# A routed-expert stage in which scatter-adds wait for those of earlier experts, and rows of x are turned and split ahead of a block's activations

## The chip, the cores and the metric

The kernel runs on one core of one Trainium2 chip. The metric is the device time of one execution in microseconds (us), lower being better. An execution is one decoder layer for 1,032 tokens, 1,024 of a new sequence and 8 single-token samples.

## The reference, cut to what matters

The layer ends with a mixture of experts: each token goes to 8 of 64 experts, and the experts' outputs are added up per token.

```python
def swiglu(x, w_gate, w_up, w_down):
    return (jax.nn.silu(x @ w_gate) * (x @ w_up)) @ w_down
...
    top_i, top_w = route(h2, p["w_router"], p["router_bias"])
    ffn = (routed_experts(h2, top_i, top_w, p["w_exp_gate"], p["w_exp_up"], p["w_exp_down"])
           + swiglu(h2, p["w_sh_gate"], p["w_sh_up"], p["w_sh_down"]))
    x = x + g2 * ffn.reshape(B, T, D)
```

D is 1024 and an expert's hidden width (FF) is 256. `routed_experts` sorts the 8,256 assignments by expert and works on blocks of 128 rows of one expert. The rows of one block, and of all blocks of one expert, are different tokens; two experts can share a token. Everything is float32. Ahead of this the layer has a conditioned norm, an input projection, two token mixers, an output projection and the routing, which the change hardly touches.

## The kernel before, in words

`routing` (to about 1055 us) finds for every expert its number of blocks. It writes `table`, which for block i holds the number of the expert (once as it is, once cut at 63), `lists`, the rows of the tokens of each block, and `xe_d`, the normed tokens with their weights in HBM. On the chip there are 92 blocks for 64 experts, so 28 blocks are not the first of their expert.

`experts` then runs all blocks in a loop that is written out by hand for each engine. The loop's code holds four blocks, and an outer loop takes eight (SPAN). Float32 products are made of three passes of rounded parts: a value is rounded to `hi`, and `lo` is what is left. So x, the gate and up weights and the first half of the down weights each need a `hi` (written by ScalarE) and a `lo` (written by VectorE). The engines work at different blocks at the same time. In the body of block i:

- GpSimd gathers the rows of block i+4 (`gather`, L2045, HBM to one of two rooms of `xg`). It then adds block i's output `ob` to `acc_d` in HBM by an indirect DMA that accumulates (L2065). Both are on GpSimd's one queue. The add waits for `ob`, for its indices `ixs`, and for the add of block i-1 to have landed (one semaphore `added`).
- TensorE transposes the hidden rows of block i (L2107, two tiles of `sg`). It transposes the x of block i+2 (`turn`, L2083, eight tiles), makes the gate and up products of block i+1 (`up`, L2092, 24 matmuls into bank 0), and then the down product of block i: six matmuls with rounded parts (L2117) and four float32 ones (L2123). The first of the six waits for `hTe_lo` and `down_lo`.
- ScalarE copies `hTe` and `hTe_hi` (L2176, L2177), writes `x_hi` of block i+2 (`take`, L2140), applies SiLU to block i+1 (`gate`, L2163), rounds the gate weights of block i+3 (L2149), the down weights of block i+1 (L2159) and the up weights of block i+3 (L2149), and writes `ob` of block i (L2185).
- VectorE writes `wexp_lo` of the up weights of block i+2 (L2207), `hTe_lo` of block i (`turned`, L2217), `x_lo` of block i+2 (`take`, L2197), and the gather's indices `ix` (L2224). It multiplies gate by up (L2221), waits for the add of block i-2 and writes `ixs` (L2227). It takes the weight column `wcol` of block i+3 from the gathered rows (L2203), and writes `wexp_lo` of the gate weights of block i+3 and `down_lo` of block i+1 (L2213).
- SyncE loads the weights of experts to come into a ring of four, 3 MB an expert.

`Final` adds the residual and norms the result once all adds have landed.

Of the kernel before, what the change touches and what calls it, by code (L numbers as in the profile page):

```python
# [25 lines left out]
D = 1024  # L26
# [14 lines left out]
E = 64  # L41
# [56 lines left out]
def layer(nc, a, o):  # L98

    with ExitStack() as top:  # L100
# [354 lines left out]
        with ExitStack() as c5:  # L455
            def far(name, shape, dt=F32):
                return sb(name, shape, dt, c5, "right")

            wdn = far("wexp_down", [P, RING, FF // P, D])
            wexp = far("wexp", [P, RING, 2, KD * FF])  # L460
            table = far("table", [1, ITEMS + AHEAD, 2], I32)
            starts = far("starts", [1, E], I32)
            total = far("total", [1, 1], I32)
            lists = far("lists", [P, ITEMS + AHEAD], U32)
            ix = [far(f"ix{b}", [P, 1], U32) for b in range(RING)]

            xg = nc.alloc_sbuf_tensor_at("xg", [P, ROOMS, XW], F32, offset=at)
            next_stage()
            up_in = [top.enter_context(nc.semaphore(f"up_in{i}")) for i in range(RING)]
            down_in = top.enter_context(nc.semaphore("down_in"))  # L470
            gat = [top.enter_context(nc.semaphore(f"gat{b}")) for b in range(RING)]
            routing(nc, tidy, a, sb, sem, banks, ident, hT, xe_d, acc_d, table, starts, total, lists, ix, xg, gat, wexp, wdn,
                    up_in, down_in)
            trunk.close()
            next_stage()
            experts(nc, tidy, a, sb, sem, banks, ident, xe_d, acc_d, table, starts, total, lists, ix, xg, gat, wexp, wdn, up_in,
                    down_in, o, eps, x2_d, mod_d)
# [1020 lines left out]
def routing(nc, tidy, a, sb, sem, banks, ident, hT, xe_d, acc_d, table, starts, total, lists, ix, xg, gat, wexp, wdn, up_in,  # L1498
# [3 lines left out]
    with ExitStack() as ctx:  # L1502
# [57 lines left out]
        with nc.Block() as block:  # L1560
# [70 lines left out]
            def _(pe):  # L1631
# [45 lines left out]
                pe.wait_ge(past_ok, 1)  # L1677
                n = ITEMS + AHEAD
                pe.matmul(banks[7][0:1, 0:n], onesb[0:E, 0:1], past[:], start=True, stop=True)
                pe.matmul(banks[7][0:1, 500:501], nbw[:, 0:1], onesb[0:E, 0:1], start=True, stop=True).then_inc(tab_ps, 1)  # L1680

                def tokens_to_places(t):
# [69 lines left out]
            def _(dve):  # L1752
# [103 lines left out]
                n = ITEMS + AHEAD  # L1856
                s.run(dve.tensor_copy(table[:, :, 0], banks[7][0:1, 0:n]))
                s.run(dve.tensor_scalar(table[:, :, 1], banks[7][0:1, 0:n], float(E - 1), None, ALU.min))
                s.run(dve.tensor_copy(total[:], banks[7][0:1, 500:501]))
                s.run(dve.tensor_copy(lists[:, ITEMS:], idle[:].to_broadcast([P, AHEAD])))  # L1860
                for t in range(2, TILES):
# [35 lines left out]
def experts(nc, tidy, a, sb, sem, banks, ident, xe_d, acc_d, table, starts, total, lists, ix, xg, gat, wexp, wdn, up_in, down_in,  # L1897
# [3 lines left out]
    with ExitStack() as ctx:  # L1901
        def tile(name, shape, dt=F32):
# [17 lines left out]
        wcol = tile("wcol", [P, RING])  # L1920
        none = tile("none", [ROW0, D // 4])
        ixs = [tile(f"ixs{b}", [P, 1], U32) for b in range(2)]
        names = "ix ixs tp xhi xlo wc whi wlo gu sg h hp h0hi h0lo h1 dhi dlo d0 dn ob scat wu pad".split()
        (ix_ok, ixs_ok, x_tp, xhi_ok, xlo_ok, wc_ok, whi_ok, wlo_ok, gu_ps, sg_ok, h_ok, h_tp, h0hi_ok, h0lo_ok, h1_ok, dhi_ok,
         dlo_ok, d0_ps, dn_ps, ob_ok, added, up_ok, pad_ok) = (sem("s6" + n) for n in names)
        passed = sem("s6passed")
        kept_in, ended = sem("s6kept"), sem("s6ended")

        def entry(eng, i, field, top):

            return eng.value_load(table[0:1, bass.ds(i, 1), field:field + 1].rearrange("a b c -> a (b c)"),  # L1931
                                  min_val=0, max_val=top)
# [28 lines left out]
        with nc.Block() as block:  # L1961
            @block.sync
            def _(sp):
# [63 lines left out]
                sp.sem_inc(ended, 1)  # L2027
                sp.wait_ge(dn_ps, n)
                sp.sem_inc(ended, 1)
                sp.wait_ge(added, 16 * n + 32)  # L2030
                sp.sem_inc(ended, 1)
                last.sync(sp)

            @block.gpsimd
            def _(pool):
                pool.memset(none[:], 0.0).then_inc(pad_ok, 1)
                pool.wait_ge(pad_ok, 1)
                for c in range(2):
                    pool.dma_start(acc_d[0:ROW0, c * (D // 2):(c + 1) * (D // 2)].rearrange("t (j n) -> t j n", j=2),
                                   none[:].unsqueeze(1).to_broadcast([ROW0, 2, D // 4])).then_inc(added, 16)  # L2040

                tidy(pool)

                def gather(j, q):
                    pool.indirect_dma_start(out=xg[:, q % ROOMS, 0:XW], out_offset=None, in_=xe_d,  # L2045
                                            in_offset=bass.IndirectOffsetOnAxis(ap=ix[q][:, 0:1], axis=0),
                                            bounds_check=LAST_ROW, oob_is_err=False).then_inc(gat[q], 16)

                for j in range(ROOMS, AHEAD):
                    pool.wait_ge(x_tp, j - 1)  # L2050
                    pool.wait_ge(wc_ok, j - 1)
                    gather(j, j)

                def block_of(i, q):
                    b = q % 2
                    pool.wait_ge(x_tp, i + 3)
                    pool.wait_ge(wc_ok, i + 3)
                    pool.wait_ge(ix_ok, i + 1)
                    pool.sem_inc(passed, 1)
                    gather(i + AHEAD, (q + AHEAD) % RING)  # L2060
                    pool.wait_ge(ob_ok, 2 * i + 4)
                    pool.wait_ge(ixs_ok, i + 1)
                    pool.wait_ge(added, 16 * i + 32)
                    pool.sem_inc(passed, 1)
                    pool.indirect_dma_start(out=acc_d, out_offset=bass.IndirectOffsetOnAxis(ap=ixs[b][:, 0:1], axis=0),  # L2065
                                            in_=ob[:, b, :], in_offset=None, bounds_check=LAST_ROW, oob_is_err=False,
                                            compute_op=ALU.add).then_inc(added, 16)

                blocks(pool, block_of)
                n = blocks_done(pool)  # L2070
                pool.wait_ge(added, 16 * n + 32)

                for q in range(RING):
                    pool.wait_ge(gat[q], 16 * ((n + AHEAD + RING - 1 - q) // RING))

            @block.tensor
            def _(pe):
# [24 lines left out]
                def block_of(i, q):  # L2102
                    b = q % 2
                    e = entry(pe, i, 1, E - 1)
                    pe.wait_ge(h_ok, i + 1)
                    for f in range(FF // P):
                        last = pe.transpose(banks[3][:, f * P:(f + 1) * P], hh[:].rearrange("p (n f) -> p f n", f=FF // P)[:, f, :], ident[:])  # L2107
                    last.then_inc(h_tp, 1)
                    turn(i + 2, (q + 2) % RING, gathered(i, q, 2))
                    up(i + 1, 1 - b)  # L2110
                    slot = e & (RING - 1)
                    pe.wait_ge(ob_ok, 2 * i + 2)
# [23 lines left out]
            def _(act):  # L2136
# [29 lines left out]
                round_weights(0, 0)  # L2166
                take(1, 1)
                round_weights(1, 1)
                gate(0)
                round_weights(2, 0)  # L2170
                round_down(0)

                def block_of(i, q):
                    b = q % 2
                    act.wait_ge(h_tp, i + 1)
                    act.activation(h1[:], banks[3][:, P:FF], ACT.Copy).then_inc(h1_ok, 1)  # L2176
                    act.activation(h0_hi[:], banks[3][:, 0:P], ACT.Copy).then_inc(h0hi_ok, 1)  # L2177
                    take(i + 2, b)
                    gate(i + 1)
                    round_weights(i + 3, 1 - b, lambda: round_down(i + 1))  # L2180
                    act.wait_ge(dn_ps, i + 1)
                    act.wait_ge(wc_ok, i + 1)
                    act.wait_ge(ixs_ok, i + 1)
                    for half in range(2):
                        act.activation(ob[:, b, 512 * half:512 * half + 512], banks[4 + half][:], ACT.Copy,  # L2185
                                       scale=wcol[:, q:q + 1]).then_inc(ob_ok, 1)
# [5 lines left out]
            def _(dve):  # L2192
# [43 lines left out]
                take(1, 1)  # L2236
                for g in range(2):
                    rest_of_weights(e, 1, 1, g)
                gate(0)
                e = entry(dve, 2, 1, E - 1)  # L2240
                weight(e, 2, 16)
                rest_of_weights(e, 2, 0, 0)
                rest_of_down(entry(dve, 0, 1, E - 1), 0)

                def block_of(i, q):
                    b = q % 2
                    rest_of_weights(entry(dve, i + 2, 1, E - 1), i + 2, b, 1)
                    turned(i)
                    take(i + 2, b)
                    to_gather(i + AHEAD, (q + AHEAD) % RING)  # L2250
                    gate(i + 1)
                    dve.wait_ge(added, 16 * i + 16)
                    dve.sem_inc(passed, 1)
                    to_add(i, b)
                    e = entry(dve, i + 3, 1, E - 1)
                    weight(e, (q + 3) % RING, gathered(i, q, 3))
                    rest_of_weights(e, i + 3, 1 - b, 0)
                    rest_of_down(entry(dve, i + 1, 1, E - 1), i + 1)

                dve.wait_ge(added, 32)  # L2260
                blocks(dve, block_of)
                dve.wait_ge(kept_in, 16 * (TILES + 3))
                last.vector(dve)
# [149 lines left out]
```

## Time and profile before

| | us |
|---|---|
| three runs | 2059.60, 2062.68, 2064.72 |
| median | 2062.68 |
| profiled execution, its own time | 2062.64 |
| its span in the profile | 2061.0 |

One line of the profile stands for a group of instructions or for one of them. Its engine is PE (TensorE matmuls), PEld (TensorE weight loads), DVE (VectorE), ACT (ScalarE), POOL (GpSimd) or SPq (SyncE's queue). The name left of the arrow is written and those right of it are read. Square brackets at the end of a row tell how long the engine had been idle before it, and what released it; "issue" means nothing that the profile shows. Matmuls overlap, so a duration of 0.39 us stands beside a distance of 0.23 us from one start to the next. In this text distances are taken from starts.

### The profile page before, as it was taken

To read this page: it belongs to the slowest core of one execution; us is meant where nothing else is said; L and a number is where in the kernel's file an instruction comes from. 1 tells how busy PE (TensorE), PEld (TensorE's weight loads), DVE (VectorE), ACT (ScalarE), POOL (GpSimd) and SP (SyncE) were. 2 spreads that over 40 slices of the span, in tenths; PEclk is the share of its full clock that TensorE was granted. 3 is DMA by queue.
4 is the path that set the end of the run, shared out by engine and by line. 5 is a ranking of instruction groups with operands and counts; after the bars stand their busy time and mean duration, and the time that the engine had idled before them with its cause. 6 is when DMAs were issued, how large, how long until landed. Compare 5 with 4: busy or idle time off the path is not lost. (4 is left out here: it accounts for less than half of the span.)

```text
span 2061.0 us, 36898 instructions
## 1 busy us (share of the span) xinstructions
PE 1908.2 (93%) x10447; PEld 1529.1 (74%) x10449; DVE 1159.2 (56%) x1714; ACT 968.8 (47%) x1395; POOL 403.8 (20%) x335
## 2 busy tenths in 40 slices
PE   4999999899899999979789999999999999999995
PEld 3999999899787666755446777777677777777772
DVE  4113401166437335446337777777777777877775
ACT  5110111244113122121246777777777777777774
POOL 0100100111111000001102223322333322333230
PEclk9999999999899999989889999999999999999998
DMA  7211311111443665324069896998998889898964
GB/s 258 73 51 41 127 47 31 32 63 61 156 134 114 238 241 195 133 93 176 27 226 298 262 346 162 325 301 294 320 310 263 269 272 300 234 348 247 313 199 177
DMA packets 181813, 399.63 MB, mean 194 GB/s; under 512 B 22137, under 2 KB 86897, under 8 KB 181758
## 3 DMA queue, kind: packets, MB, share of 16 engines
q1 hardware_dynamic: 149166, 312.16, 42.5%
q0 software_dynamic: 31392, 82.49, 15.7%
q10 hardware_dynamic: 1200, 4.26, 0.6%
q8 instruction: 33, 0.54, 0.1%
q14 instruction: 22, 0.18, 0.0%
HBM read 350.16 MB, written 80.64 MB: 209 GB/s over the span
## 5 line engine op out<-in xcount | busy, mean ns | idle before, releaser
L2207 DVE TENSOR_TENSOR wexp_lo<-wexp,wexp_hi 128x2048 fp32r<-128x2048 f32 x189 | 432.7, 2290 | 81.5 <-ACT wexp_hi L2149 45.7
L2149 ACT ACTIVATE wexp_hi<-wexp 128x2048 fp32r x190 | 362.0, 1907 | 47.5 <-issue 45.7
L2092 PE MATMUL bank<-wexp_hi,x_hi 128*128 128x512 f32 x744 | 300.1, 403 | 3.8 <-DVE wexp_lo L2207 3.8
L2092 PE MATMUL bank<-wexp_hi,x_lo 128*128 128x512 f32 x744 | 292.0, 392 | 0.0
L2092 PE MATMUL bank<-wexp_lo,x_hi 128*128 128x512 f32 x744 | 290.7, 391 | 0.0
L2065 POOL DMA_INDIRECT acc_d<-ob,ixs x92 | 165.4, 1798 | 578.3 <-DMA acc_d<-ob,ixs 477.0
L548 PE MATMUL bank<-hT_hi,w_hi 128*128 128x344 f32 x576 | 187.5, 326 | 7.3 <-DVEq L660 7.3
L548 PE MATMUL bank<-hT_hi,w_lo 128*128 128x344 f32 x576 | 185.3, 322 | 0.0
L548 PE MATMUL bank<-hT_lo,w_hi 128*128 128x344 f32 x576 | 184.7, 321 | 0.0
L2123 PE MATMUL bank<-wexp_down,hTe 128*128 x368 | 173.2, 593 | 0.0
L2092 PEld LDWEIGHTS bank<-wexp_hi,x_lo 128*128 128x128 f32 x744 | 140.3, 189 | 31.0
L2092 PEld LDWEIGHTS bank<-wexp_hi,x_hi 128*128 128x128 f32 x744 | 140.5, 189 | 30.2 <-issue 4.2
L2092 PEld LDWEIGHTS bank<-wexp_lo,x_hi 128*128 128x128 f32 x744 | 140.8, 189 | 27.1
L2045 POOL DMA_INDIRECT xg<-xe_d,ix x94 | 131.1, 1395 | 83.9 <-DVE wcol L2203 46.7
L711 PE MATMUL bank<-hT_hi,wg_hi 128*128 128x344 f32 x384 | 129.6, 337 | 12.8 <-POOLq L118 6.7
L634 DVE TENSOR_TENSOR w_lo<-w_raw,w_hi 128x1024 fp32r<-128x1024 f32 x27 | 33.1, 1226 | 186.6 <-POOL w_hi L538 170.3
L711 PE MATMUL bank<-hT_lo,wg_hi 128*128 128x344 f32 x384 | 124.7, 325 | 0.0
L711 PE MATMUL bank<-hT_hi,wg_lo 128*128 128x344 f32 x384 | 124.5, 324 | 0.0
L2163 ACT ACTIVATE sg<-bank 128x256 f32<-128x256 f32 x93 | 35.8, 385 | 180.6 <-PE bank L2092 174.8
L2197 DVE TENSOR_TENSOR x_lo<-bank,x_hi 128x512 fp32r<-128x512 f32 x188 | 120.2, 681 | 0.6 <-ACT x_hi L2140 0.6
L2213 DVE TENSOR_TENSOR down_lo<-wexp_down,down_hi 128x1024 fp32r<-128x1024 f32 x93 | 113.4, 1219 | 4.8 <-ACT down_hi L2159 4.8
L2083 PE MATMUL bank<-ident,xg 128*128 128x128 f32 x752 | 99.6, 276 | 17.1 <-DMA xg<-xe_d,ix 11.4
(365 smaller groups left out, 3458.6 us busy)
## 6 DMA issues: line engine op xcount, KB each, us to landing
wexp<-in_w_exp_gate SPq DMA_DIRECT2D x128, 512.0 KB
wexp<-in_w_exp_up SPq DMA_DIRECT2D x128, 512.0 KB
wexp_down<-in_w_exp_down SPq DMA_DIRECT2D x128, 512.0 KB
wada<-in_w_ada SPq DMA_DIRECT2D x12, 2048.0 KB, 10.8
w_raw<-in_w_in SPq DMA_DIRECT2D x44, 512.0 KB, 3.9
gates_d<-gst POOLq DMA_DIRECT2D x48, 172.0 KB, 2.1
gate<-gates_d SPq DMA_DIRECT2D x16, 516.0 KB, 5.6
xn<-in_x_prompt ACTq DMA_DIRECT2D x8, 512.0 KB, 8.1
```

What stands on the lines that cost most here:

```text
L548: last = pe.matmul(bank, stat(k), mov(k), start=(k == 0 and x == 0), stop=(k == KD - 1 and x == 2))
L711: last = pe.matmul(banks[7][:, 0:PIECE], stat[j][:, k, :], mov[:, k, toks], start=(k == 0 and x == 0), stop=(k == KD - 1 and x == 2))
L2045: pool.indirect_dma_start(out=xg[:, q % ROOMS, 0:XW], out_offset=None, in_=xe_d, in_offset=bass.IndirectOffsetOnAxis(ap=ix[q][:, 0:1], axi ...
L2065: pool.indirect_dma_start(out=acc_d, out_offset=bass.IndirectOffsetOnAxis(ap=ixs[b][:, 0:1], axis=0), in_=ob[:, b, :], in_offset=None, bou ...
L2083: last = pe.transpose(banks[1 + k // 4][:, (k % 4) * P:(k % 4 + 1) * P], xg[:, q % ROOMS, k * P:(k + 1) * P], ident[:])
L2092: last = pe.matmul(banks[0][:].rearrange("p (g n) -> p g n", g=2), stat[:, b, k, :], mov[:, b, :, k * FF:(k + 1) * FF], start=(k == 0 and ...
L2123: last = pe.matmul(banks[4 + half][:], h1[:], wdn[:, bass.ds(slot, 1), 1, half * 512:half * 512 + 512].rearrange("p a n -> p (a n)"), star ...
L2149: act.activation(w_hi[:, b, g, :], wexp[:, bass.ds(e & (RING - 1), 1), g, :].rearrange("p a n -> p (a n)"), ACT.Copy).then_inc(whi_ok, 1)
L2163: act.activation(sg[:], banks[0][:, 0:FF], ACT.Silu).then_inc(sg_ok, 1)
L2197: dve.tensor_tensor(x_lo[:, b, at, :].rearrange("p k n -> p (k n)"), banks[1 + half][:], x_hi[:, b, at, :].rearrange("p k n -> p (k n)"), ...
L2207: dve.tensor_tensor(w_lo[:, b, g, :], wexp[:, bass.ds(e & (RING - 1), 1), g, :].rearrange("p a n -> p (a n)"), w_hi[:, b, g, :], ALU.subtr ...
L2213: dve.tensor_tensor(d0_lo[:], down_first(e), d0_hi[:], ALU.subtract).then_inc(dlo_ok, 1)
```

## The change

It has four parts.

1. **Adds.** `added` becomes two semaphores, one for the blocks with even numbers and one for those with odd ones. The table gets a third number for each block: how many blocks lie before the first block of its expert (one more matmul and one more copy in `routing`). GpSimd reads it from the table in each block. It lets an add wait only for the adds of the other parity that belong to earlier experts. The add of the same parity two blocks earlier is still waited for by VectorE ahead of `ixs`.
2. **First block.** The first half of the down weights of block 0 is rounded ahead of the first `gate` on ScalarE and on VectorE, where it was rounded last ahead of the loop.
3. **TensorE.** In a block, `turn` comes ahead of the transposes of the hidden rows.
4. **ScalarE and VectorE.** In a block, `take` comes ahead of `hTe` and `hTe_hi` on ScalarE, and ahead of `turned` (`hTe_lo`) on VectorE.

```diff
+                pe.matmul(banks[7][0:1, n:2 * n], nbw[:, 0:1], past[:], start=True, stop=True)
...
+                s.run(dve.tensor_copy(table[:, :, 2], banks[7][0:1, n:2 * n]))
...
+        added = [sem(f"s6scat{b}") for b in range(2)]
...
-                    pool.wait_ge(added, 16 * i + 32)
+                    pool.wait_ge(added[1 - b], ((entry(pool, i, 2, ITEMS) + b) >> 1) * 16 + 16)
...
-                                            compute_op=ALU.add).then_inc(added, 16)
+                                            compute_op=ALU.add).then_inc(added[b], 16)
...
                     e = entry(pe, i, 1, E - 1)
+                    turn(i + 2, (q + 2) % RING, gathered(i, q, 2))
                     pe.wait_ge(h_ok, i + 1)
...
                     last.then_inc(h_tp, 1)
-                    turn(i + 2, (q + 2) % RING, gathered(i, q, 2))
                     up(i + 1, 1 - b)
...
+                round_down(0)
                 gate(0)
                 round_weights(2, 0)
-                round_down(0)
 
                 def block_of(i, q):
                     b = q % 2
+                    take(i + 2, b)
                     act.wait_ge(h_tp, i + 1)
                     act.activation(h1[:], banks[3][:, P:FF], ACT.Copy).then_inc(h1_ok, 1)
                     act.activation(h0_hi[:], banks[3][:, 0:P], ACT.Copy).then_inc(h0hi_ok, 1)
-                    take(i + 2, b)
                     gate(i + 1)
...
+                rest_of_down(entry(dve, 0, 1, E - 1), 0)
                 gate(0)
...
-                rest_of_down(entry(dve, 0, 1, E - 1), 0)
...
                     rest_of_weights(entry(dve, i + 2, 1, E - 1), i + 2, b, 1)
+                    take(i + 2, b)
                     turned(i)
-                    take(i + 2, b)
                     to_gather(i + AHEAD, (q + AHEAD) % RING)
                     gate(i + 1)
-                    dve.wait_ge(added, 16 * i + 16)
+                    dve.wait_ge(added[b], (i - b) * 8 + 16)
```

VectorE, in a block of the loop, before. Names stand as in the list above; `x2` at the end of a row is a pair.

```order
L2207 TENSOR_TENSOR wexp_lo<-wexp,wexp_hi 128x2048
L2216 REGISTER_ALU
L2217 TENSOR_TENSOR hTe_lo<-bank,hTe_hi 128x128
L2197 TENSOR_TENSOR x_lo<-bank,x_hi 128x512 x2
L2224 ISA
L2224 COPY ix<-lists 128x1
L2221 TENSOR_TENSOR sg<-sg,bank 128x256
```

The same place of VectorE with the change, whose line numbers are 7 higher here:

```order
L2214 TENSOR_TENSOR wexp_lo<-wexp,wexp_hi 128x2048
L2203 REGISTER_ALU
L2204 TENSOR_TENSOR x_lo<-bank,x_hi 128x512 x2
L2223 REGISTER_ALU
L2224 TENSOR_TENSOR hTe_lo<-bank,hTe_hi 128x128
L2231 ISA
L2231 COPY ix<-lists 128x1
L2228 TENSOR_TENSOR sg<-sg,bank 128x256
```

The pair of `x_lo` has moved ahead of `hTe_lo`; nothing else in the block of VectorE has moved.

GpSimd, between the gather and the add of one block, with the change. L1934 is the read of the table's third number, L2068 the wait for the adds.

```order
L2050 DMA xg<-xe_d,ix 128x1088 [waits x_in4]
L2066 ISA
L1934 ISA [waits x_in3,w_ready]
L1934 TENSOR_LOAD table
L1934 ISA x2
L2068 ISA
L2070 DMA acc_d<-ob,ixs 1033x1024 [waits ss_ps]
```

Before, no load of the table stood between the two DMAs; gather and add keep their order.

## Rows read from the trace of the kernel before

**Rows 1.** The page: the span and the granted clock in 40 slices.

```profile
span 2061.0 us, 36898 instructions
...
PEclk9999999999899999989889999999999999999998
```

**Rows 2.** Transposes of hidden rows (L2107), two a block: count, duration, first and last start.

```profile
L2107 PE MATMUL bank<-ident,sg x184: 272/279/391, 1075.6 to 2001.6; 128*128 128x128 f32 x184
```

**Rows 3.** One block in order of time: start, duration, engine, line, tile.

```profile
1430.85 0.39 PE L2117 MATMUL bank<-down_hi,hTe_hi 128*128 128x512 f32 x1
...
1431.05 0.38 ACT L2163 ACTIVATE sg<-bank 128x256 f32<-128x256 f32 x1 [1.77 <-PE bank L2092]
...
1431.92 1.91 ACT L2149 ACTIVATE wexp_hi<-wexp 128x2048 fp32r x1 [0.49 <-issue]
...
1433.92 0.39 PE L2107 MATMUL bank<-ident,sg 128*128 128x128 f32 x2
1434.07 2.29 DVE L2207 TENSOR_TENSOR wexp_lo<-wexp,wexp_hi 128x2048 fp32r<-128x2048 f32 x1 [0.92 <-ACT wexp_hi L2149]
1434.15 1.04 PE L2083 MATMUL bank<-ident,xg 128*128 128x128 f32 x8
...
1436.28 1.22 DVE L2213 TENSOR_TENSOR down_lo<-wexp_down,down_hi 128x1024 fp32r<-128x1024 f32 x1
...
1437.41 2.29 DVE L2207 TENSOR_TENSOR wexp_lo<-wexp,wexp_hi 128x2048 fp32r<-128x2048 f32 x1
...
1437.95 1.10 ACT L2140 ACTIVATE x_hi<-bank 128x512 fp32r<-128x512 f32 x2
...
1439.61 0.28 DVE L2217 TENSOR_TENSOR hTe_lo<-bank,hTe_hi 128x128 fp32r<-128x128 f32 x1
...
1439.81 1.28 DVE L2197 TENSOR_TENSOR x_lo<-bank,x_hi 128x512 fp32r<-128x512 f32 x2
...
1440.51 0.39 PE L2117 MATMUL bank<-down_hi,hTe_hi 128*128 128x512 f32 x1
...
1441.01 0.14 DVE L2224 COPY ix<-lists 128x1 uint32 x1
```

**Rows 4.** Who waited for whom, 1066 to 2016 us: total, times, longest.

```profile
POOL acc_d L2065 <- DMA acc_d<-ob,ixs: 477.0, 73, 9.7
...
POOL acc_d L2065 <- ACT ob L2185: 74.8, 15, 6.0
...
PE bank L2083 <- DMA xg<-xe_d,ix: 11.4, 14, 1.9
```

**Rows 5.** Add, gather and what waits for it, in order of time.

```profile
1504.84 1.58 POOL L2065 DMA_INDIRECT acc_d<-ob,ixs  x1 [6.20 <-DMA acc_d<-ob,ixs]
1506.72 1.05 POOL L2045 DMA_INDIRECT xg<-xe_d,ix  x1 [0.31 <-issue]
...
1515.35 1.58 POOL L2065 DMA_INDIRECT acc_d<-ob,ixs  x1 [7.57 <-DMA acc_d<-ob,ixs]
1516.40 0.39 PE L2107 MATMUL bank<-ident,sg 128*128 128x128 f32 x2
...
1517.24 1.09 PE L2083 MATMUL bank<-ident,xg 128*128 128x128 f32 x8 [0.45 <-DMA xg<-xe_d,ix]
```

**Rows 6.** Around the first passage of the loop, in order of time.

```profile
1080.40 1.23 DVE L2213 TENSOR_TENSOR down_lo<-wexp_down,down_hi 128x1024 fp32r<-128x1024 f32 x1 [0.46 <-ACT down_hi L2159]
...
1086.48 0.77 PE L2117 MATMUL bank<-down_hi,hTe_hi 128*128 128x512 f32 x1 [3.97 <-issue]
```

**Rows 7.** Where VectorE comes from one passage of eight blocks to the next.

```profile
1249.71 0.73 PE L2117 MATMUL bank<-down_hi,hTe_hi 128*128 128x512 f32 x1 [2.26 <-issue]
1250.24 0.63 PE L2117 MATMUL bank<-down_lo,hTe_hi 128*128 128x512 f32 x1
...
1491.31 2.29 DVE L2207 TENSOR_TENSOR wexp_lo<-wexp,wexp_hi 128x2048 fp32r<-128x2048 f32 x1 [2.36 <-issue]
1493.52 0.28 DVE L2217 TENSOR_TENSOR hTe_lo<-bank,hTe_hi 128x128 fp32r<-128x128 f32 x1
...
1493.90 0.47 PE L2117 MATMUL bank<-down_hi,hTe_hi 128*128 128x512 f32 x1 [2.23 <-issue]
```

**Rows 8.** The last add, behind its `ob`.

```profile
2013.68 1.24 ACT L2185 ACTIVATE ob<-bank,wcol 128x512 f32<-128x512 f32 x2
2015.89 1.58 POOL L2065 DMA_INDIRECT acc_d<-ob,ixs  x1 [5.34 <-ACT ob L2185]
```

**Rows 9.** DMA over a fifth of the loop: PE, PEld, DVE, ACT, POOL, clock, DMA share, GB/s.

```profile
1786.00:1966.00 180.00, 174.51 (x782) 132.20 (x781) 136.82 (x176) 134.64 (x180) 58.67 (x37) 1.00 0.91 295
```

More of the change, by code:

```diff
@@ L460, in layer @@
             wexp = far("wexp", [P, RING, 2, KD * FF])
-            table = far("table", [1, ITEMS + AHEAD, 2], I32)
+            table = far("table", [1, ITEMS + AHEAD, 3], I32)
             starts = far("starts", [1, E], I32)
@@ L1922, in experts @@
         ixs = [tile(f"ixs{b}", [P, 1], U32) for b in range(2)]
-        names = "ix ixs tp xhi xlo wc whi wlo gu sg h hp h0hi h0lo h1 dhi dlo d0 dn ob scat wu pad".split()
+        names = "ix ixs tp xhi xlo wc whi wlo gu sg h hp h0hi h0lo h1 dhi dlo d0 dn ob wu pad".split()
         (ix_ok, ixs_ok, x_tp, xhi_ok, xlo_ok, wc_ok, whi_ok, wlo_ok, gu_ps, sg_ok, h_ok, h_tp, h0hi_ok, h0lo_ok, h1_ok, dhi_ok,
-         dlo_ok, d0_ps, dn_ps, ob_ok, added, up_ok, pad_ok) = (sem("s6" + n) for n in names)
+         dlo_ok, d0_ps, dn_ps, ob_ok, up_ok, pad_ok) = (sem("s6" + n) for n in names)
         passed = sem("s6passed")
+        added = [sem(f"s6scat{b}") for b in range(2)]
         kept_in, ended = sem("s6kept"), sem("s6ended")
@@ L2029, in _ @@
                 sp.sem_inc(ended, 1)
-                sp.wait_ge(added, 16 * n + 32)
+                sp.wait_ge(added[0], ((n + 1) >> 1) * 16 + 16)
+                sp.sem_inc(passed, 1)
+                sp.wait_ge(added[1], (n >> 1) * 16 + 16)
                 sp.sem_inc(ended, 1)
@@ L2039, in _ @@
                     pool.dma_start(acc_d[0:ROW0, c * (D // 2):(c + 1) * (D // 2)].rearrange("t (j n) -> t j n", j=2),
-                                   none[:].unsqueeze(1).to_broadcast([ROW0, 2, D // 4])).then_inc(added, 16)
+                                   none[:].unsqueeze(1).to_broadcast([ROW0, 2, D // 4])).then_inc(added[c], 16)
                 tidy(pool)
@@ L2066, in block_of @@
                                             in_=ob[:, b, :], in_offset=None, bounds_check=LAST_ROW, oob_is_err=False,
-                                            compute_op=ALU.add).then_inc(added, 16)
+                                            compute_op=ALU.add).then_inc(added[b], 16)
                 blocks(pool, block_of)
                 n = blocks_done(pool)
-                pool.wait_ge(added, 16 * n + 32)
+                pool.wait_ge(added[0], ((n + 1) >> 1) * 16 + 16)
+                pool.sem_inc(passed, 1)
+                pool.wait_ge(added[1], (n >> 1) * 16 + 16)
                 for q in range(RING):
@@ L2258, in block_of @@
                     rest_of_down(entry(dve, i + 1, 1, E - 1), i + 1)
-                dve.wait_ge(added, 32)
+                dve.wait_ge(added[0], 16)
+                dve.wait_ge(added[1], 16)
                 blocks(dve, block_of)
```

## The prediction

> **What bounds the kernel now.** I read the page first, for the span and the clock [rows 1]: TensorE is at its full 2.4 GHz nearly throughout. The change lives in the expert loop, so I then took the starts of the hidden rows' transposes, two a block [rows 2]. From the first to the last block they span 926.0 us, 91 distances from block to block. The shape of a block comes from the view in order of time [rows 3]. Let E be the end of the up product (which is when the down product of the block can start), and D the actual start of the down product. In [rows 3] both are 1430.85, and the next are 1440.51: 9.66 us of TensorE work without a wait. Starting points repeat at that distance in about half of the blocks. 91 x 9.66 = 879 us, so 47 us of the 926 are waits. By a list of all 92 blocks, made with the distances of [rows 3] as the norm, 5.5 lie in the first block [rows 6], some 17 at `turn`, where the gathered rows are late (14 waits with 11.4 us are named in [rows 4]; [rows 5] show one, 0.84 us from hidden transposes to `turn` where [rows 3] have 0.23), 12 ahead of the down product, 9 where one block gives way to the next, and the rest is clock and small change.
>
> Two things stand close behind TensorE. **The first** is the chain of the adds: 73 of the 92 waited for the add before them, 477 us in all [rows 4]. In [rows 5] one add follows the other after 10.51 us, and the gather stands behind the add on GpSimd's queue. So a late add makes a late gather, and that makes TensorE wait. **The second** is VectorE's way to `hTe_lo`, and on it the change acts most. In [rows 3] follow E = 1430.85: SiLU at 1431.05, rounding at 1431.92, `wexp_lo` at 1434.07, `down_lo`, the second `wexp_lo` at 1437.41, and `hTe_lo`, which ends at 1439.89. That is E + 9.04, against 9.66 for TensorE: 0.62 us to spare. The down product starts about 0.10 us after `hTe_lo` where that is what it waits for (1493.80 to 1493.90 in [rows 7]). In my list the time from the end of `hTe_lo` to the down product is 0.6 us or more in 34 blocks, 0.2 to 0.6 in 35, and 0.10 to 0.14, so that TensorE waited, in 23.
>
> **Part 4, x_lo ahead of hTe_lo.** The pair of `x_lo` takes 1.20 us of VectorE (1439.81 to the next start at 1441.01, [rows 3]), and `hTe_lo` now comes that much later. `x_hi` doesn't hold it up: with `take` first, ScalarE would have it done before the second `wexp_lo` ends at 1439.70, since today it begins at 1437.95 and takes 1.10 [rows 3]. `x_lo` itself is wanted a block later, so its being early is worth nothing. The down product can then start at E + 9.04 + 1.20 + 0.10 = E + 10.34. But not every block pays the whole 0.68 over 9.66. ScalarE's chain starts from E, not from D. If a block's down product is late by s, the next E is late by s as well, and the next down product has only 0.68 - s left to wait. Two neighbours together wait 0.68, so two blocks take 10.34 + 9.66 = 20.00 and one 10.00: **+0.34 us a block, 91 x 0.34 = +31 us.** Blocks whose `hTe_lo` is late already (23 of them) can't share: they pay 1.20 instead of the pair's 0.68, **23 x 0.52 = +12 us**. The upper bound is no sharing and no slack, 92 x 1.2 = 110; the lower is nothing if the pair found idle time of VectorE, for which [rows 3] leave no room between 1434.07 and 1441.01. ScalarE's part of the move costs nothing: `hTe_hi` ends 1.10 later, at about 1439.2, still ahead of the second `wexp_lo`'s end.
>
> **Part 3, turn first.** Same work. `turn` starts 0.23 us earlier, and so do its readers, which don't hurry. Where the gather is late, the hidden transposes used to run inside that wait and now come behind it: 14 waits x 0.23 = at most +3, and less, as gathers become less late.
>
> **Part 1, adds.** 28 of the 92 blocks are not the first of their expert, and only their adds are freed. Each lets the chain catch up by whatever it lags: singles fall behind by 10.51 - 9.66 = 0.85 a block, or 0.5 against the new pace of 10.00, and every second or third block is a free one. So I let nearly all late gathers go: **-17 us**, and with them 3 of the 12 us ahead of the down product, **-3**. What is late next is `hTe_lo`. The bounds are 0 (see the DMA rival) and -47 (all waits gone). The new read of the table costs GpSimd something between `ob` and the add. No row shows it there. The nearest is the 0.49 us idle of ScalarE before its rounding, where it loads from the table too [rows 3]; the other end is 0, since an add that waits for another has its load behind it. It counts once, at the last add, which had only its `ob` to wait for and began 0.97 us after that [rows 8]: **+0.5**. The matmul and the copy in routing are at most one transposed tile pair and one column copy, 0.39 + 0.14 [rows 3]: **+0.3**.
>
> **Part 2, first block.** `down_lo` of block 0 (1.23 us and 0.46 of waiting [rows 6]) leaves VectorE's way to the first down product, and `x_lo` (1.20) comes onto it: **-0.5**.
>
> **Clock.** At the change from one passage of eight blocks to the next, VectorE sometimes idles 2.4 us [rows 7]. After a 2.26 us gap TensorE went on at half its clock (0.43 us between down matmuls, 1250.24 on, against 0.23; 1.2 GHz instead of 2.4), after one of 2.23 it did not [rows 7]. These gaps become 1.2 longer, and each event costs 6 x 0.20 = 1.3 us: two more such events, **+2.5**, between 0 and 11 x 1.3 = 14. By the page "TensorE: Matmul & The Clock Gate" of the Trainium skill (section "HAM oscillation — how this bites in real kernels"), gaps of idleness put the engine back at the lower clock; by that rule each of the 11 would be a sure loss and this term its upper end.
>
> **Sum:** 31 + 12 + 2 - 20 + 0.5 + 0.3 - 0.5 + 2.5 = +28. The terms overlap (a block that waits for its gather is mostly one of the 23), so I take 5 off: **+23 us.** The profiled execution took 2062.64, practically the median of the runs (2062.68), so 2086.
>
> **The rivals.** *A: the adds were the true bound, and the kernel gets faster.* For it: the chain of adds covers 73 of 92 blocks [rows 4], and early gathers let VectorE start its work on time. It decides if the freed adds bring more than `x_lo` costs, which needs `hTe_lo` to end within E + 9.56 even with `x_lo` ahead. Gain 17 to 20 with nothing given back: 2062.6 - 18 = 2045. Against it: VectorE is late in [rows 3] though the gather was early enough, since ScalarE's rounding is what it waits for at 1434.07. *B: the two cancel or hide each other,* +-6, at 2062. This is also the case that the freed adds gain 20 and only the late blocks lose. *C: freeing adds gains nothing,* because the DMA engines are 0.91 busy [rows 9], and two adds in flight only take longer each. Then the 20 stay away: 2086 + 17 = 2103. The page "DMA: Bandwidth & Descriptors" of the Trainium skill (section "Issuing engines are not separate DMA queues") speaks for it: transfers, whoever starts them, run on the same 16 engines and interleave. Against it: at 10.00 us a block the gathers have more time anyway, so part of the gain comes even then.
>
> **How the numbers follow.** Forecast 0.66, A 0.12, B 0.10, C 0.12. A measurement of this kernel can tell about 0.3%, 6.2 us, from no change. Faster is A, 0.12; the same is B, 0.10; slower is the forecast and C, 0.78. For the range I leave out A and the upper end of C. The low end is the forecast with the gather gain doubled and the late blocks free, 2086 - 17 - 12 = 2057; the high end is C with a little less, 2102.
>
> **What would show it.** Right: the median distance of blocks rises from 9.66 to about 10.0, often as a short and a long one in turn. The down product (now L2124) waits in most blocks, 0.1 us behind `hTe_lo`, with 30 us or more in all. The adds' wait for adds falls well below 477 us, and `turn` hardly waits for the gather. Wrong: `hTe_lo` ends by E + 9.6 in most blocks; or distances of 9.66 prevail; or `turn` still waits as often as now.

## The result, and the profile after

| | before | changed |
|---|---|---|
| median | 2062.53 | 2085.84 |
| lowest to highest of 4 runs | 2059.60 to 2064.72 | 2084.25 to 2087.21 |
| span of the profiled execution | 2061.0 | 2083.1 |

The ratio is 1.0111 with a 95% interval of 1.0095 to 1.0127: the change makes the kernel 23.3 us slower. Medians in this text are of fast runs: one run of e6 (2790.98 us) and one of the kernel before beside e9 to e12 (3894.29 us) were in a far slower state and are left out.

The page of the changed kernel, and its chain of waits. The clock is as before ([rows 1]). The chain by lines no longer starts with the adds, which had 19% of the span before (the last row below is of the kernel before):

```profile
span 2083.1 us, 37459 instructions
...
PEclk9999999999899999989889999999999999999997
...
PE 39%; DMA 5%; issue 3%; DVE 1%; ACT 1%; ACTq 0%; SPq 0%; DVEq 0%; POOLq 0%; POOL 0%
PE bank L2099 21%; PE bank L2130 6%; PE bank L2124 6%; PE bank L2090 4%; DMA wexp_down<-in_w_exp_down 3%; DMA acc_d<-ob,ixs 1%; PE bank L2115 1%; PE bank L2324 1%; DMA xg<-xe_d,ix 1%; ACTq L1934 0%; DVE yy L2386 0%; PE bank L2329 0%; DVE wexp_lo L2214 0%; ACT ob L2192 0%; ACT wexp_hi L2156 0%
...
DMA acc_d<-ob,ixs 19%; PE bank L2092 9%; DMA xg<-xe_d,ix 4%; PE bank L2123 2%; PE bank L2117 2%; PE bank L2083 2%; DVEq L1931 1%; DVE wexp_lo L2207 1%; ACT wexp_hi L2149 1%; PE bank L2316 1%; ACTq L1931 0%; POOLq L1931 0%; DVE yy L2378 0%; ACT ob L2185 0%; PE bank L2107 0%
```

The hidden transposes, the counterpart of [rows 2] (count, duration, first and last start):

```profile
L2115 PE MATMUL bank<-ident,sg x184: 279/283/389, 1075.7 to 2021.0; 128*128 128x128 f32 x184
```

From the first to the last block it takes 945.3 us instead of 926.0. So 19.3 us arose in the loop, 0.1 ahead of its first hidden transposes, and 2.7 behind its last ones (62.1 us to the end of the span instead of 59.4). The distances from block to block changed as follows:

| | before | changed |
|---|---|---|
| median distance | 9.72 | 10.40 |
| below 9.75 us | 47 of 91 | 20 of 91 |
| above 10.3 us | 27 | 47 |
| down product starts 0.10 to 0.14 us behind `hTe_lo` | 23 of 92 | 60 of 92 |

From 1671 on, for instance, they run 9.7, 10.5, 9.7, 10.6, 9.7, 10.5: a long and a short one in turn. The list of who waited for whom, 1066 to 2040 us, against [rows 4]:

```profile
POOL acc_d L2070 <- issue: 314.3, 48, 9.7
POOL acc_d L2070 <- DMA acc_d<-ob,ixs: 301.2, 44, 9.0
...
PE bank L2124 <- issue: 30.4, 46, 3.4
...
PE bank L2090 <- issue: 12.0, 12, 1.8
```

L2124 is the down product: 30.4 us of waiting in 46 places, all put down to "issue" since the profile sees no single releaser of its three semaphores. L2090 is `turn`, whose 12 waits are at the ends of passages. Adds are named as waiting for adds in 44 blocks instead of 73. But GpSimd's idle time ahead of the adds has not fallen: 314.3 us of it in 48 blocks now have no releaser that the profile names (26 us in 4 blocks before). What most of these adds wait for can be read from their own `ob`: 64 of the 92 adds start at most 1.9 us behind its end, 1.7 to 1.8 us in nearly all of them, where before 17 did, 16 of them at 1.0 us. They wait for `ob` and then for the read of the table. One block in order of time shows the cause of the longer time, the counterpart of [rows 3]:

```profile
1635.00 0.39 PE L2124 MATMUL bank<-down_hi,hTe_hi 128*128 128x512 f32 x1
...
1635.20 0.38 ACT L2170 ACTIVATE sg<-bank 128x256 f32<-128x256 f32 x1 [3.05 <-PE bank L2099]
...
1636.31 1.91 ACT L2156 ACTIVATE wexp_hi<-wexp 128x2048 fp32r x1 [0.72 <-issue]
...
1638.45 2.29 DVE L2214 TENSOR_TENSOR wexp_lo<-wexp,wexp_hi 128x2048 fp32r<-128x2048 f32 x1 [1.28 <-ACT wexp_hi L2156]
...
1641.79 2.28 DVE L2214 TENSOR_TENSOR wexp_lo<-wexp,wexp_hi 128x2048 fp32r<-128x2048 f32 x1
...
1643.99 1.28 DVE L2204 TENSOR_TENSOR x_lo<-bank,x_hi 128x512 fp32r<-128x512 f32 x2
...
1645.19 0.28 DVE L2224 TENSOR_TENSOR hTe_lo<-bank,hTe_hi 128x128 fp32r<-128x128 f32 x1
...
1645.57 0.47 PE L2124 MATMUL bank<-down_hi,hTe_hi 128*128 128x512 f32 x1 [0.74 <-issue]
```

From E = 1635.00, `hTe_lo` ends at 1645.47, and the down product starts 0.10 us later, 10.57 us behind E. The prediction said 10.34. This block is 0.23 late of its own, by ScalarE's gap ahead of its rounding (0.72 us here, 0.49 in [rows 3] and in most blocks of both kernels). In most blocks `hTe_lo` ends at E + 10.25 and the down product starts at E + 10.35, as predicted. Two neighbours show how they share the wait:

```profile
1303.43 0.39 PE L2124 MATMUL bank<-down_hi,hTe_hi 128*128 128x512 f32 x1
...
1313.40 0.28 DVE L2224 TENSOR_TENSOR hTe_lo<-bank,hTe_hi 128x128 fp32r<-128x128 f32 x1
...
1313.78 0.47 PE L2124 MATMUL bank<-down_hi,hTe_hi 128*128 128x512 f32 x1 [0.52 <-issue]
...
1323.09 0.28 DVE L2224 TENSOR_TENSOR hTe_lo<-bank,hTe_hi 128x128 fp32r<-128x128 f32 x1
...
1323.56 0.39 PE L2124 MATMUL bank<-down_hi,hTe_hi 128*128 128x512 f32 x1
```

The first down product starts at its E, 1303.43. The second starts 10.35 us later, 0.68 us behind its own E (1313.10). The third waits for nothing: its E has moved back with the second, 9.78 us behind it, and its `hTe_lo` ended 0.19 us earlier. The two distances make 20.13 us, where the prediction had 20.00. From block to block the waits run 0.68, 0, 0.82, 0, 0.68, 0 there.

I compared where TensorE's steps stand further apart than their usual distance, summed over the loop. Ahead of the down product it is 39.1 us instead of 16.1 (+23.0). From the down product to the next block it is 18.0 instead of 9.2 (+8.8). Between hidden transposes, `turn` and `up` it is 2.4 instead of 18.5, without the start (-16.1). Within the down product it is 6.9 instead of 4.9 (+2.0). Together +17.7. The rest of the 19.3 is 0.01 to 0.02 us a block on the usual distances themselves.

### The profile page after: what moved, and what is told of

It is laid out like the page before. It is cut to its first block and busy times, and to the rows that moved or that the text cites. A ratio compares the mean times of both kernels' runs of the same rounds, so it can differ in the third digit from the quotient of the medians.

```text
span 2083.1 us, 37459 instructions
## 1 busy us (share of the span) xinstructions
PE 1918.8 (92%) x10449; PEld 1520.0 (73%) x10450; DVE 1160.8 (56%) x1715; ACT 968.9 (47%) x1395; POOL 377.4 (18%) x335
## 5 line engine op out<-in xcount | busy, mean ns | idle before, releaser
L2070 POOL DMA_INDIRECT acc_d<-ob,ixs x92 | 168.5, 1832 | 615.5 <-issue 314.3
L2090 PEld LDWEIGHTS bank<-ident,xg 128*128 128x128 f32 x752 | 86.8, 142 | 74.1 <-issue 73.6
L2050 POOL DMA_INDIRECT xg<-xe_d,ix x94 | 102.0, 1085 | 92.7 <-DVE ixs L2234 34.3
L2090 PE MATMUL bank<-ident,xg 128*128 128x128 f32 x752 | 99.5, 276 | 18.4 <-issue 12.0
```

What stands on the lines that cost most here:

```text
L2090: last = pe.transpose(banks[1 + k // 4][:, (k % 4) * P:(k % 4 + 1) * P], xg[:, q % ROOMS, k * P:(k + 1) * P], ident[:])
```

## The experiments

Three theories stood at the start. **Theory 1**: `x_lo` ahead of `hTe_lo` on VectorE costs, the freed adds gain. **Rival 2**: the new wait with its table read, or `turn` first, costs. **Rival C** of the prediction: freed adds gain nothing, because the DMA engines are full. Each comparison has runs of the kernel before on the same chip.

| run | what it is | median, us | ratio to before, 95% interval |
|---|---|---|---|
| e1 | changed, VectorE's order back | 2051.74 | 0.9958 (0.9944 to 0.9972) |
| e2 | before, VectorE's order alone | 2087.68 | 1.0130 (1.0113 to 1.0148) |
| e3 | before, adds alone | 2053.06 | 0.9960 (0.9941 to 0.9980) |
| e4 | changed, adds back | 2085.81 | 1.0118 (1.0102 to 1.0135) |
| e5 | changed, half of `x_lo` ahead | 2064.95 | 1.0011 (1.0000 to 1.0022) |
| e6 | changed, half an `x_lo` more ahead | 2113.12 | 1.0252 (1.0226 to 1.0278) |
| e7 | before, TensorE's order alone | 2064.33 | 1.0011 (0.9998 to 1.0024) |
| e8 | parts 1 and 2, `hTe_lo` first | 2055.27 | 0.9956 (0.9940 to 0.9971) |
| e9 | parts 1 and 2 | 2049.93 | 0.9930 (0.9902 to 0.9959) |
| e10 | before, `hTe_lo` first | 2062.35 | 0.9989 (0.9973 to 1.0005) |
| e11 | e9, gather ahead of the add | 2051.48 | 0.9937 (0.9912 to 0.9963) |
| e12 | e11, `hTe_lo` first | 2047.75 | 0.9922 (0.9892 to 0.9952) |

The runs of before had medians of 2061.31 (e1 to e4), 2062.12 (e5 to e8) and 2064.4 (e9 to e12).

**e1, VectorE's order back in the changed kernel.**

```diff
                     rest_of_weights(entry(dve, i + 2, 1, E - 1), i + 2, b, 1)
-                    take(i + 2, b)
                     turned(i)
+                    take(i + 2, b)
```

> The changed kernel with VectorE's order alone as before: hTe_lo ahead of x_lo. Theory 1 (x_lo ahead of hTe_lo on VectorE is what costs): the 39 us of waits ahead of the down product fall to about 12, most distances from block to block go back to 9.66 us, and the freed adds show their gain: 2040 to 2055 us. Rival 2 (the adds' new wait and table read, or turn first on TensorE, are what costs): stays within 5 us of 2086. Rival 3 (half and half): about 2070.

2051.74 us, 34 us under the changed kernel (32 by the two ratios, which have different runs of before), with the waits ahead of the down product at 13.1 us. In the profiles 29.6 us of it lie in the loop (915.7 us instead of 945.3) and 3.8 ahead of the loop, where e1 changes nothing. What the change costs lies in these two lines.

**e2, the same two lines alone, swapped in the kernel before.**

> The kernel before with VectorE's order alone changed: x_lo ahead of hTe_lo. Theory 1: +31 for the pairs and +12 for late blocks, less what late gathers lose at the slower pace (5 to 15): 2090 to 2100 us, and distances of 9.7 and 10.6 us in turn. Rival 2: no more than 5 us over 2062.

2087.68, 26 us over before, with ScalarE and TensorE in their old order: rival 2 is out. It came a little under the theory's range, and its list of waits shows one reason:

```profile
POOL acc_d L2065 <- DMA acc_d<-ob,ixs: 461.8, 67, 8.9
...
PE bank L2117 <- issue: 37.2, 49, 5.2
...
PE bank L2083 <- DMA xg<-xe_d,ix: 0.8, 2, 0.5
```

The adds still wait for each other in 67 blocks, yet `turn` waits 0.8 us for gathered rows instead of 11.4. The slower pace alone gives the gathers the time they need.

**e3, the adds alone (all of part 1 put into the kernel before).**

> The kernel before with part 1 alone (two semaphores, a table entry more, adds wait for those of earlier experts). Theory 1: 14 to 20 us faster than before, 2043 to 2049, with the waits of turn for gathered rows nearly gone. Theory that the DMA engines are the bound (C): within 4 us of before. Rival 2: slower than before by 5 or more.

2053.06, 8 us faster, half of what was expected. The waits for gathers did go (from 17.1 us, measured as distances, to 3.9). But the block-to-block step grew by 0.7 us and the wait ahead of the down product by 1.3. Some of what is won at the gather is lost at the next wait. In the profile the loop is 12.0 us shorter (914.0 instead of 926.0), but that run, at 2049.07 us, was one of the faster ones of six from 2046.66 to 2058.08.

**e4, the adds as before in the changed kernel.** The diff is part 1 taken out.

> The changed kernel with the adds as before: one semaphore, each add waits for the one before it. By the term of the prediction (20 us gained by freed adds whatever the rest does): 2103 us. If the slower pace of 10.0 us a block already gives the adds time: 2086 to 2092. Rival 2: faster than 2080.

2085.81 against 2085.84, and a ratio of 1.0118 against 1.0111, whose intervals overlap: the freed adds bring nothing here that can be told from noise, which could hide some 5 us. With the adds as before `turn` waits 0.5 us for gathered rows. The term of -17 us was right in size and had the wrong owner.

**e5 and e6, less and more ahead of `hTe_lo`.** These test the rule that two neighbours share the wait.

```diff
-                    take(i + 2, b)
+                    take(i + 2, b, (0,))
                     turned(i)
+                    take(i + 2, b, (1,))
```

In e6 half an `x_lo` is written once more ahead of the pair:

```diff
+                    dve.wait_ge(xhi_ok, 2 * (i + 2) + 1)
+                    dve.tensor_tensor(x_lo[:, b, 0:4, :].rearrange("p k n -> p (k n)"), banks[1][:],
+                                      x_hi[:, b, 0:4, :].rearrange("p k n -> p (k n)"), ALU.subtract).then_inc(extra, 1)
+                    dve.wait_ge(extra, i + 1)
                     take(i + 2, b)
                     turned(i)
```

> The changed kernel with the first half of x_lo ahead of hTe_lo and the second half behind it. If two neighbouring blocks share the wait: hTe_lo can end at E + 9.64, the pair waits 0.08 us instead of 0.68, so only blocks that are late already pay (about 20 x 0.5): 2058 to 2065 us, nearer to the 2052 of the order put back than to 2086. If every block pays in proportion to what stands ahead: halfway, 2069 or more.

> The changed kernel with one more x_lo half (written twice, with a wait between) ahead of hTe_lo, about 0.7 us more. Sharing: two blocks take 0.7 longer, 91 x 0.35 = 32, and late ones the whole: 2115 to 2125 us. No sharing: 91 x 0.7 = 64, 2145 or more. If VectorE had idle time left ahead of hTe_lo: 2086 to 2095.

Both are near what sharing says and far from its rivals: e5 at 2064.95, the upper end of its range, and e6 at 2113.12, 2 us under it. The hidden transposes of e6:

```profile
L2116 PE MATMUL bank<-ident,sg x184: 279/282/384, 1074.3 to 2050.0; 128*128 128x128 f32 x184
```

The loop takes 975.7 us instead of 945.3: 30.4 more, 0.33 us a block. In most blocks `hTe_lo` now ends at E + 10.98 instead of E + 10.25, 0.73 us later, so about half of what was put in is paid, and the waits run 1.40, 0, 1.40, 0. And e5, with half of the 1.2 us, costs 13 us over e1 (11 by the ratios), while the second half costs 21: the price rises once the slack is used up. In e5 `hTe_lo` ends at E + 9.65, and the waits run 0.08, 0.

**e7, TensorE's order alone.** The diff is part 3.

> The kernel before with turn ahead of the hidden transposes on TensorE, nothing else. The prediction's term: 0 to +3 us, 2061 to 2065. Rival, from the runs so far: where one passage of eight blocks gives way to the next, turn comes about 0.8 us later behind the down product than the hidden transposes did (11 places), so +6 to +9 us, 2067 to 2071.

2064.33, a ratio of 1.0011 with 1 inside the interval. The rival of 6 to 9 us is wrong; late gathers cost `turn` 15.0 us in this run. The row from the changed kernel that had suggested it is this one:

```profile
1244.77 1.09 PE L2090 MATMUL bank<-ident,xg 128*128 128x128 f32 x8 [1.77 <-issue]
```

Such gaps between passages of eight blocks also grew in e2 (from 9.2 to 16.7 us in all), which has the old order on TensorE. In e1, which has `turn` first and `hTe_lo` in time, `turn` waits 8.7 us at ends of passages, against 12.0 in the changed kernel. So the gaps go with a late `hTe_lo` and not with `turn`. Why is open: whether TensorE reads its instructions less far ahead of the loop's end when it is held up at the down product was not tried.

**e8 and e10, `hTe_lo` moved the other way**, with freed and with old adds.

```diff
-                    rest_of_weights(entry(dve, i + 2, 1, E - 1), i + 2, b, 1)
                     turned(i)
+                    rest_of_weights(entry(dve, i + 2, 1, E - 1), i + 2, b, 1)
                     take(i + 2, b)
```

> The kernel before with part 1 (adds) and part 2 (first block), and with VectorE's hTe_lo moved the other way: ahead of the second wexp_lo. Theory 1: the time between the end of hTe_lo and the down product grows from 0.6 to about 2 us, the 13 to 17 us of waits ahead of the down product fall to under 4: 2036 to 2044 us. Rival: x_lo, gate product and weight column come later on VectorE and something else waits: no faster than 2052.

> The kernel before, with hTe_lo ahead of the second wexp_lo on VectorE, adds as before. If the wait for hTe_lo was a limit of its own: 12 us faster, 2050. If it only hid the late gathers (as in e8, where its waits went and gathers at turn rose from 4 to 20 us): within 4 us of before, 2058 to 2066, with over 20 us of late gathers at turn.

`hTe_lo` now has 2.1 us to spare in most blocks, and the waits directly ahead of the down product fell to 2.5 us (e8) and 1.6 (e10). Neither gained: e8 is no faster than e9 below, which is the same kernel without this move, and e10 is as before. The rival expectation of e8 and the second one of e10 came true (20.4 us of late gathers at `turn` in e10). The list of waits of e8:

```profile
ACT down_hi L2166 <- DMA wexp_down<-in_w_exp_down: 28.8, 11, 4.4
PE bank L2090 <- DMA xg<-xe_d,ix: 14.7, 17, 2.5
PE bank L2114 <- DVE sg L2228: 12.2, 11, 1.3
```

The pace is not the reason that gathers are late here: e9 has the same median distance of 9.66 us and waits 2.6 us for them. The order on VectorE is. `hTe_lo` now holds up the second `wexp_lo`, and what stands behind that comes about 1.5 us later than in e9: `ix`, `ixs` and the gate product start 8.7, 9.1 and 8.7 us behind the hidden transposes (medians) instead of 7.1, 7.6 and 7.2. GpSimd then issues the gather 1.4 us later, 10.3 us instead of 11.4 ahead of its `turn`, and a gather takes 9.5 us to land. The later gate product `sg` holds up the hidden transposes. Down weights are waited for 28.8 us, against 24.5 in e9.

**e9, parts 1 and 2 alone.**

> The kernel before with parts 1 and 2 alone (adds, first block); TensorE, ScalarE and VectorE keep their order in a block. From e3 (adds alone, 8 us faster than before) and part 2's way to the first down product (down_lo 1.7 us earlier, x_lo not in its way): 8 to 11 us faster than before, 2051 to 2054. If turn first had been of use in e1: slower than e1's ratio of 0.9958.

2049.93. This is the change without what costs: 36 us under the changed kernel. Against e1 it lacks part 3 and ScalarE's half of part 4, and the two can't be told apart. Here the landing of every add can be read too: 19 of the 92 adds start before the one ahead of them has landed, where in e7 and e10, with the adds as before, none does. Against e3 it has part 2 more: the distance from the first to the second hidden transposes is 11.3 us instead of 15.8.

**e11 and e12, the gather ahead of the add on GpSimd's queue**, without and with `hTe_lo` first.

```diff
-AHEAD = 4
+AHEAD = 5
...
-                    pool.wait_ge(x_tp, i + 3)
-                    pool.wait_ge(wc_ok, i + 3)
-                    pool.wait_ge(ix_ok, i + 1)
+                    pool.wait_ge(x_tp, i + 4)
+                    pool.wait_ge(wc_ok, i + 4)
+                    pool.wait_ge(ix_ok, i + 2)
```

One more semaphore, `rooms`, lets TensorE release the gather of the last block, behind its own loop.

> As e9, and each gather stands ahead of the add on GpSimd's queue instead of behind it (it fetches block i+5 in body i, as soon as turn has freed the room). If late gathers come from standing behind the adds: waits of turn for gathers and of VectorE's wcol nearly vanish, 2040 to 2048 us. If they come from the DMA engines being full: no faster than e9.

> As e11, and hTe_lo ahead of the second wexp_lo on VectorE. If gathers are no longer late, VectorE's slack of 2 us at hTe_lo makes it the fastest: 91 x 9.66 = 879 for the blocks, some 15 us of ends of passages and late weights: 2028 to 2040 us. If the DMA engines are the bound: as e11 and e8, 2050.

Nothing on TensorE or VectorE is named as waiting for a gather any more in either, so late gathers did come from standing behind the adds. And still they take 2051.48 and 2047.75. Part of the reason lies behind the loop. These are GpSimd's last two instructions of the loop in e11:

```profile
2004.58 1.04 POOL L2051 DMA_INDIRECT xg<-xe_d,ix  x1 [13.04 <-issue]
2006.17 1.58 POOL L2074 DMA_INDIRECT acc_d<-ob,ixs  x1 [0.55 <-issue]
```

The gather of the last block fetches rows that nobody needs. It is released only when TensorE has left its loop, and the last add stands behind it on the queue: it starts 8.4 us behind the end of its `ob` in e11 and 6.6 in e12, against 1.7 in e9 and in e8, and the final stage waits for it. In e11 the loop is 4.0 us shorter than in e9 (910.9 instead of 914.9) and what follows it 6.9 us longer; in e12 the loop is 9.8 us shorter than in e8 and what follows it 3.3 us longer. Without this late add I estimate 2045 and 2043 us, from these differences of 6.7 and 4.9 us; that was not run. So e11 does not show that its gain failed for want of DMA. The rest of the reason is other waits. The list of e12:

```profile
POOL acc_d L2074 <- DMA acc_d<-ob,ixs: 206.8, 54, 6.3
...
ACT down_hi L2173 <- DMA wexp_down<-in_w_exp_down: 46.4, 17, 4.8
...
PE bank L2119 <- DVE sg L2235: 20.3, 20, 1.3
```

ScalarE waits 46.4 us for down weights, against 28.8 in e8 and 14.9 in the kernel before. In e11 it waits 26.6, hardly more than in e9 (24.5). A window of 900 us of e11, columns as in [rows 9]:

```profile
1066.00:1966.00 900.00, 879.69 (x3947) 673.48 (x3946) 691.87 (x896) 670.76 (x892) 267.34 (x177) 0.99 0.90 292
```

The DMA engines are 0.90 busy at 292 GB/s; in the kernel before they are 0.88 busy at 287 in the same window. Whether the weights come later in e12 because the gathers do, or are only wanted sooner at its faster pace, was not tried. By its median e12 is the fastest of all, but its interval overlaps with that of e9, so no more can be said than that both beat the two kernels of this study.

## Why the prediction was right, and where it was not

The forecast was 2086 us, and 2085.84 was measured. The mechanism was the one given. Not all of its terms hold, and that the sum came out to 0.2 us is luck: the waits ahead of the down product were put 12 us too high, and the steps from block to block and the time behind the loop, together 11 us more, too low.

- **`x_lo` ahead of `hTe_lo`: right.** e1 and e2 put 34 and 26 us on it alone. The down product starts 0.10 us behind `hTe_lo` in 60 blocks, at the predicted E + 10.35, and long and short distances take turns. Sharing between neighbours is seen in the waits of 0.68 and 0 in turn, and e6 (0.33 us a block for 0.73) and the bend between e5 and e1 bear it out.
- **The size of that term, +31 and +12: too large.** The waits ahead of the down product grew by 23.0 us, and the steps from block to block, which no term named, by 8.8. Together +32, against +43 less the 3 for late blocks and the 5 for overlap. The pairs were sized well: outside the first block the waits are 36.2 us, where pairs of 0.68 and 0 alone make 31. It is the +12 for late blocks that failed. Their waits, 11.7 us before, were not added to the pairs' but more than half taken up by them.
- **"So I let nearly all late gathers go: -17", put down to the freed adds: the step that failed.** The waits did go (-16 us), but in e2 they went without part 1, and e4 shows part 1 worth nothing in the changed kernel. Its worth depends on the pace: 8 us at the old one (e3), none that can be told from noise at the new one. The prediction noted under rival C that the gathers have more time at 10.00 us a block, and did not draw the conclusion. Its sign that the adds' wait for adds would fall well below 477 us is met by name only (301.2 us); in sum the adds wait as long as before, now mostly for `ob`.
- **Rival C, 2103 us: wrong as a time.** It took the gathers for as late at the slow pace as at the fast one. Its ground, that the DMA engines are nearly full, is not shown to be a bound by any run here: the late gathers of e8 come from VectorE's order, and e11 lost its gain to the last add. The rule of the Trainium skill's page "DMA: Bandwidth & Descriptors" (section "Issuing engines are not separate DMA queues") is that all transfers share the 16 engines. No run here sets it apart from other causes: with the gathers put forward, the waits for down weights rose in e12 (28.8 to 46.4 us) and hardly in e11 (24.5 to 26.6).
- **Rival A, the adds as the true bound: wrong** for the change as a whole, and half right for part 1 alone.
- **Clock, +2.5: about right in size, wrong in cause.** No further block fell to the lower clock. The down products of blocks 0 and 16 had it before, and only that of block 0 with the change. The premise failed: the gaps of 2.26 and 2.23 us did not become 1.2 longer; in the same places they are 0.28 and 1.79, and behind the second the clock stayed full:

```profile
1500.72 0.47 PE L2124 MATMUL bank<-down_hi,hTe_hi 128*128 128x512 f32 x1 [1.79 <-issue]
1501.03 0.39 PE L2124 MATMUL bank<-down_lo,hTe_hi 128*128 128x512 f32 x1
1501.26 0.40 PE L2124 MATMUL bank<-down_hi,hTe_lo 128*128 128x512 f32 x1
```

  So the loss at each of the 11 passage ends, which the prediction had as the upper end of this term, came at none: gaps as long as it feared did not arise there. (The six steps of 0.20 make 1.2 and not 1.3.) What grew, by 2.0 us, is the first distance of a down product that has waited, 0.31 us instead of 0.23, in 60 blocks instead of 20: 3.2 us, less some 1.3 for block 16.

- **First block, -0.5:** the distance from first to second hidden transposes fell from 15.3 to 15.1. That small sum hides two large parts: without `x_lo` ahead of `hTe_lo`, part 2 shortens it by 4.4 us (e9 against e3). **The table read, +0.5:** the last add starts 2.92 us after its `ob` begins, instead of 2.21 ([rows 8]): 0.7 us. The other 2 us behind the loop vary by as much from kernel to kernel (58.6 to 63.1 us from the last hidden transposes to the end in e1 to e10), and stay open. So does the time ahead of the loop (first hidden transposes from 1071.5 to 1076.2).

## What to carry to other kernels

In a software pipeline, look up how long ahead of its reader each write ends, before two instructions of one engine change places: here one that a matmul waited for with 0.62 us to spare went behind 1.2 us of work that was wanted a block later. Follow the added delay around the loop too: where the late chain starts from the end of a product and not from the delayed instruction, two blocks share one delay, and half of it is paid. And value a removed wait at the pace that the kernel will have: freed adds were worth 8 us at 9.7 us a block and nothing that could be measured at 10.4. Look at the stretches ahead of, in and behind a loop one by one: in e11 4 us won in the loop were lost to one add behind it.

## What the runs showed of the hardware that was not expected

Gaps of TensorE between two passages of the outer loop follow how early its last wait in the block is met, though no instruction there has changed. From the start of the down product to the next block's transposes, over the usual 3.07 us, the 11 ends of passages sum to 2.6 us in e10 (`hTe_lo` ends 2.1 us early), 8.5 before (0.4 us early in the median block) and 14.6 in e2 (waited for in most blocks).

The length of a gap alone did not tell whether the clock would fall. Between down matmuls the distance is 0.23 us at 2.4 GHz and 0.43 at 1.2 GHz. Behind gaps of 1.93 us (e11, at 1486.4) and 2.04 us (e3, at 1488.7) it was at the lower level within two matmuls; behind 2.35 us (e1, at 1723.5) and 2.77 us (e5, at 1083.7) all six stayed at the full one.

A matmul of the down product that had waited was followed by the next after 0.31 us instead of 0.23, at the full clock.
